# Weight low parts of the mixers' tiles: subtracted on VectorE at the end of a step, instead of on GpSimd beside it

## The reference, cut to what matters

```
h = rms_norm(x) * (1 + scale1) + shift1
h @ w_in -> A: pooling mixer (256), B: neighbourhood attention (8 heads x 64),
            C: gated linear attention (4 heads, dk 32, dv 64)
x = x + gate1 * concat(A, B, C) @ w_out
x = x + gate2 * swiglu(rms_norm(x) * (1 + scale2) + shift2)
```

## Time and profile before

| | |
|---|---|
| median of 3 runs | 1757.54 us (1757.44 to 1759.84) |
| the profiled execution | 1757.72 us; its span, first to last instruction, 1755.9 us |
| TensorE matmul | busy 1678.0 us (96%) |
| VectorE | 1038.4 us (59%) |
| GpSimd | 585.4 us (33%), of it 499.6 us the 196 subtractions of line 536 |
| ScalarE | 558.6 us (32%) |
| mean granted clock of TensorE | 0.98 |

### The profile page before, as it was taken

How to read it: one execution, slowest core, us unless ns; L and a number is a source line. 1 busy time by engine, 2 the same in 40 slices (tenths; PEclk the granted TensorE clock), 3 DMA queues, 4 the chain that set the end, 5 groups by cost and what they waited for, 6 DMA issues and landing times. The chain is left out here.

```text
span 1755.9 us, 29168 instructions
## 1 busy us (share of the span) xinstructions
PE 1678.0 (96%) x12024; PEld 1610.0 (92%) x12024; DVE 1038.4 (59%) x1885; ACT 558.6 (32%) x910; POOL 585.4 (33%) x281
## 2 busy tenths in 40 slices
PE   5979999999999999999999789998999999999998
PEld 4878889889999999999998678897999999999998
DVE  3477455758887488528777855566677713331342
ACT  4322455343322122112343225444332212221221
POOL 1135111126333334333452421111544333333332
PEclk9889899999999999999999989998999999999999
DMA  9234312112443344334331011210233222222223
GB/s 366 73 130 157 104 63 72 53 37 96 137 150 125 127 144 143 97 96 150 110 118 61 15 40 67 67 67 25 81 102 117 96 72 72 74 81 74 72 63 105
DMA packets 51306, 171.01 MB, mean 97 GB/s; under 512 B 6352, under 2 KB 9232, under 8 KB 51088
## 3 DMA queue, kind: packets, MB, share of 16 engines
q1 hardware_dynamic: 51216, 169.81, 29.5%
HBM read 165.98 MB, written 3.80 MB: 97 GB/s over the span
## 5 line engine op out<-in xcount | busy, mean ns | idle before, releaser
L536 POOL TENSOR_TENSOR w_lo<-w_raw,w_hi 128x1024 fp32r<-128x1024 f32 (+2 forms) x196 | 499.6, 2550 | 1083.9 <-ACT w_hi L637 1050.2
L637 ACT ACTIVATE w_hi<-w_raw 128x1024 fp32r<-128x1024 f32 (+2 forms) x194 | 200.3, 1033 | 674.2 <-PE acc L1367 609.9
L1367 PE MATMUL acc<-h_lo,w_hi 128*128 128x320 f32 (+1 forms) x1456 | 335.3, 312 | 0.0
L1367 PE MATMUL acc<-h_hi,w_hi 128*128 128x320 f32 (+1 forms) x1456 | 335.2, 312 | 0.0
L1367 PEld LDWEIGHTS acc<-h_hi,w_hi 128*128 128x128 f32 x1456 | 246.6, 190 | 1.6 <-issue 1.3
L1367 PEld LDWEIGHTS acc<-h_lo,w_hi 128*128 128x128 f32 x1456 | 246.3, 189 | 0.0
L1367 PE MATMUL acc<-h_hi,w_lo 128*128 128x320 f32 (+1 forms) x1456 | 230.3, 310 | 0.0
L1367 PEld LDWEIGHTS acc<-h_hi,w_lo 128*128 128x128 f32 x1456 | 219.7, 189 | 0.0
L1225 DVE SCALAR_TENSOR_TENSOR x<-acc,mods,x 128x320 f32<-128x320 f32 (+2 forms) x192 | 72.6, 434 | 221.9 <-PE acc L1367 200.9
L1367 PE MATMUL acc<-y_lo,w_hi 128*128 128x320 f32 x808 | 183.9, 309 | 0.0
L1367 PE MATMUL acc<-y_hi,w_hi 128*128 128x320 f32 x808 | 183.9, 309 | 0.0
(11 more groups left out here) (245 smaller groups left out, 2200.1 us busy)
## 6 DMA issues: line engine op xcount, KB each, us to landing
w_raw<-in_w SPq DMA_DIRECT2D x176, 512.0 KB, 3.5
mod_w<-in_w_ada SPq DMA_DIRECT2D x56, 512.0 KB, 4.5
w_gm<-in_w_ada SPq DMA_DIRECT2D x24, 512.0 KB, 4.6
bias<-in_bias SPq DMA_DIRECT2D x16, 576.0 KB, 4.6
w_ada<-in_w_ada SPq DMA_DIRECT2D x16, 512.0 KB, 13.6
w_raw<-in_w SPq DMA_DIRECT2D x16, 384.0 KB, 3.1
x<-in_x SPq DMA_DIRECT2D x4, 640.0 KB, 9.4
out_x<-x SPq DMA_DIRECT2D x8, 320.0 KB, 3.9
```

What stands on the lines that cost most here:

```text
L536: pool.tensor_tensor(w_lo[p][:, 0:n], raw[p][:, 0:n], w_hi[p][:, 0:n].bitcast(F32), ALU.subtract).then_inc(lo_made[p], 1)
L637: act.activation(w_hi[p][:, 0:n], raw[p][:, 0:n], ACT.Copy).then_inc(hi_made[p], 1)
L1367: mm = pe.matmul(acc[p][:, half, 0:m.shape[-1]], w[:, k * P:(k + 1) * P], m, start=w is w_hi[p] and k == 0 and part is hi, stop=w is w_lo[ ...
```

## The change

In the mixers `low` of tiles 8 to 23 leaves GpSimd's program and is put into VectorE's loop, in the steps that have a tile done, at the end of the step: only the pooling sums of steps 44 and 47 come behind it. It waits there for ScalarE's copy `w_hi` of the same tile, which ScalarE makes in the same step. Tiles 0 to 7 and those from 24 on stay on GpSimd. GpSimd's copies by head keep their order and their waits, without a subtraction between them.

```diff
--- before
+++ after
@@ GpSimd
-                for t in range(T_OUT):
+                for t in range(T_PAIR + 2):
                     low(t)
-                    if t == T_PAIR + 1:
-                        if l == 0:
-                            pool.wait_ge(late_in, 16 * NLATE)
-                        q_by_head(0)
-                        states_by_head(0)
-                        q_by_head(1)
-                    if t == T_PAIR + 2:
-                        for j in range(1, NP):
-                            if j + 1 < NP:
-                                q_by_head(j + 1)
-                            states_by_head(j)
-                low(T_OUT)
-                low(T_OUT + 1)
+                if l == 0:
+                    pool.wait_ge(late_in, 16 * NLATE)
+                q_by_head(0)
+                states_by_head(0)
+                q_by_head(1)
+                for j in range(1, NP):
+                    if j + 1 < NP:
+                        q_by_head(j + 1)
+                    states_by_head(j)
@@ VectorE
+                def low(t):
+
+                    p, n = t % 2, kts_of(t) * P
+                    dve.wait_ge(hi_made[p], slot_uses(l, t) + 1)
+                    dve.tensor_tensor(w_lo[p][:, 0:n], raw[p][:, 0:n], w_hi[p][:, 0:n].bitcast(F32),
+                                      ALU.subtract).then_inc(lo_made[p], 1)
...
+                    for n in tiles_done(g):
+                        low(T_PAIR + n + 2)
                     for i in range(2):
                         if g == 44 + 3 * i:
                             window_sums(i)
```

## The result

The kernel after takes 1738.63 us (median of 4 runs, 1737.44 to 1741.12) against 1757.76 for the kernel before on the same chip (4 runs, 1757.44 to 1759.84): ratio 0.9891, 95% interval 0.9873 to 0.9908. The forecast was 1737.0, with a range of 1730 to 1751. The profiled execution took 1737.4 with a span of 1735.7, 20.2 less than the 1755.9 of before.

What follows compares the result with a forecast made beforehand. TensorE was taken as the bound, full in attention, losing time to stalls on VectorE, held up by GpSimd's subtractions, and to half clock after them. 1757.7 - 4.0 - 3.5 - 3.2 - 10.0 = 1737.0 us; range 1730 to 1751.

Steps and rivals of the forecast that it cites:

- Step 9: Linear attention's norm, freed from GpSimd's subtractions, takes some 4.1 for 8.07; TensorE resumes 4.0 us earlier (layer 0), 3.5 (layer 1).
- the two stall terms: Shorter TensorE waits in linear attention: 4.0 us in layer 0, 3.5 in layer 1 after 0.5 off for step 4.
- Pooling sums: Before the first pooling product: window sums take 0.86 for 2.14; 1.6 us of the 3.22 stall per layer, 3.2 in all.
- The price of step 4: Linear attention: the low delays kk's multiply 2.1 us; 0.5 us left on layer 1's path, none in layer 0.
- The 32 lows: VectorE, mostly attention and pooling: 1.22 us each, 39 us more work; those of attention and pooling cost nothing, 32 us without cover.
- Rival two: Attention: VectorE becomes the bound, TensorE waits at each of 26 lows; slower, 1769 us; chance 0.06.
- Rival three: Step 7: head copies hold up the low, 2.44 for 1.22, step-4 wait back in full; 1741 to 1745; chance 0.15.
- DMA: Tile loads that wait for the lows: over 10 us sooner for tile 9, about a microsecond either way elsewhere; none late.
- Clock: Four half-clock stretches, in linear attention and pooling, recover 10.0 us of at most 15.3.
- rival one: Linear attention and pooling: stalls shrink but the clock does not recover; only 10.7 us come, 1747; chance 0.25.
- two thirds of the bound: Share taken of the 15.3 us that the four half-clock stretches cost at most: 10.0 us.

Runs made afterwards that it cites:

- e4: Kernel before, nothing moved to VectorE; GpSimd waits with the lows of tiles 9 and 10 until step 9's norm is done: 1747.1 us, ratio 0.9948.
- e5: Kernel after, plus three idle GpSimd subtractions with two SBUF inputs behind the head copies, where step 9's norm runs: 1750.6 us, ratio 0.9959.
- e6: Kernel after, plus six GpSimd memsets behind the last head copies, which write SBUF and do not read it: 1741.0 us, ratio 0.9900.
- e10: Kernel after once more, unchanged, with a second trace: 1739.3 us, ratio 0.9889.
- e8: Kernel after, lows of steps 4 and 7 put a step later on VectorE, those of 44 and 47 behind the window means: 1741.8 us, ratio 0.9905.
- e7: Kernel after, each low of steps 14 to 40 done twice on VectorE, once into a dead tile: 1739.6 us, ratio 0.9891.
- e11: Kernel after, plus twelve idle TensorE products in the wait for layer 1's second score product: 1736.4 us, ratio 0.9873.
- e12: Kernel of e9, plus seven idle TensorE products in the wait for layer 1's second score product: 1731.8 us, ratio 0.9860 to the kernel before.
- e1: Kernel before, only the lows of tiles 9 and 10 moved to VectorE (4 of 32): 1751.2 us, ratio 0.9963.
- e9: Kernel before, all lows on GpSimd, which waits with tiles 9, 10 for step 9's norm and 20, 21 for the window means: 1737.8 us, ratio 0.9876.

## Why the prediction was right, point by point

**Step 9: contention, 4.0 + 3.5.** Right, and shown from three sides: the norm is short when GpSimd is told to wait (e4), long again when it reads idle data (e5: 2.86 and 2.84), and short when it only writes (e6). The norm takes 4.09, forecast were some 4.1. The waits lost 8.8 (8.0 in e10, the second trace), against 8.0 in the two stall terms without the 0.5 that was taken off for step 4. In the kernel before neither of the two waits for the other there, so engines meet in SBUF too, and not only through semaphores. The Trainium skill's rule (SBUF — State Buffer, Who interferes with whom) has it so: a VectorE instruction with two SBUF inputs contends with a GpSimd instruction that reads SBUF, and not with one that only writes it. The traces agree on both halves, 2.86 us in e5 and 0.82 in e6.

**Pooling sums, 1.6 per layer.** Right: L1101 takes 0.86 in all four. The first bias add behind the first sum comes 0.95 sooner than the one before it had, the one behind the second 0.71 more: 1.66, against 0.9 and 0.7. TensorE's wait is 1.9, not 1.6: it lost 1.3 and not 1.6, since TensorE comes 0.3 sooner.

**The price of step 4, 0.5 in layer 1.** Right. The second score product starts 14.71 us after the first state update, where it was 12.63 (971.89 to 984.52): 2.1 later, as reckoned. The third starts after 23.95 instead of 23.53 (985.33 and 995.42): 0.4 of it is left. e8 undid this and gained nothing. What the prediction did not see is that VectorE is held up by GpSimd ahead of this wait too (last section).

**The 32 lows, nothing.** Right: 1.22 us each, attention unchanged at 127.9, and unchanged with nine more in each layer (e7). Rival two falls. Rival three's 2.44 did not come; a low beside the head copies takes 1.53 at most, and the wait that step 7's low brings is 0.7.

**DMA, nothing.** Right by the waits: no transfer of a tile is among those that grew, and TensorE's wait for GpSimd's lows went from 2.3 to 1.7.

**Clock, 10.0.** Too large: the parts show 5 to 8. That the total came out all the same was in part luck. At the four places that the term was added up from, the missing clock fell by 10.1 us, but they were not all that there was: the four parts had 27.2 us of it and kept 19.1. Of the 10.0, some 5.5 were for the poolings, where TensorE's busy time fell by 5.0 (5.1 in e10), and some 4.5 for linear attention, where it fell by 0.3 (0.1 in e10). The rest was filled by two waits that the sum does not have, for `mods` (2.8) and `gla_o` (1.5). The first is chance: in e10, the same kernel, it is 3.4 again.

The reason given for the term holds in part. That half clock goes with TensorE's standing still is shown for one wait (e11, e12). That only stalls of 3.22 us and more bring it is not so. In the kernel after, the clock is 1.00 from 982 to 990 us and then falls, with TensorE busy throughout and no wait since 976.09:

```profile
990.00:1000.00 10.00, 10.00 (x89) 8.84 (x89) 8.32 (x15) 5.11 (x7) 6.03 (x7) 0.83 0.08 13
```

Nor does the length of a wait tell how much follows: e8's 3.82 us brought more half clock than after's 5.89. The pooling wait of 1.9 us was followed by pooling parts of 53.9, 55.5 and 57.1 us in kernels with the same code there (after, e6, e7, e10). And rival one is what e1 showed, a stall of 8.0 us gone and in sum no clock back. What calls the half clock where TensorE does not wait stays open. The term should have stood with a spread of several us in every execution; two thirds of the bound fitted the poolings and not linear attention.

## What to carry to other kernels

Where an elementwise instruction takes three times as long in one place as in another, look at what the other elementwise engine reads just then. The cure need not be to move the work: a wait that keeps the two apart gave the same time here (e9). An engine with idle time under a full TensorE takes more work for nothing (e7); that a piece gains by standing behind what TensorE waits for next is not shown, since e8 did that and gained nothing. Time that a clock gives back should be forecast with a wide range, and a total that comes out right should be taken apart into busy and idle time before its terms are believed. A long TensorE wait that can't be removed may be worth filling with idle products: the medians fell by 2.9 us (e11) and 6.1 us (e12 against e9).

## What the runs showed that was not expected

The change cured the contention at two places, and a third is left: step 4 of linear attention, whose wait of 5.89 us is the longest in the mixers now. VectorE's arguments of kk and GpSimd's copies by head in layer 1 of the kernel after, in order of time:

```profile
965.87 3.39 DVE L999 TENSOR_TENSOR kk<-bcum 128x256 f32<-128x256 f32 x4
969.29 1.41 DVE L1003 TENSOR_SCALAR kk<-kk 128x1024 f32<-128x1024 f32 x1
...
976.32 1.42 DVE L999 TENSOR_TENSOR kk<-bcum 128x256 f32<-128x256 f32 x4
977.78 0.69 DVE L1003 TENSOR_SCALAR kk<-kk 128x1024 f32<-128x1024 f32 x1
```

```profile
965.11 2.69 POOL L559 TENSOR_TENSOR s_heads<-states,heads 128x256 f32<-128x256 f32 x4 [11.38 <-DVE states L1031]
967.76 2.40 POOL L546 TENSOR_TENSOR q_heads<-z,heads 128x512 f32<-128x512 f32 x2
```

Beside the copies the two lines take 4.8 us, 2.7 more than a chunk later, when GpSimd is idle. No run keeps the two apart here, so what that would be worth is not shown. The wait for `mods` in layer 0 hangs on the same thing: `mods` is made behind these two lines. They took 3.39 and 1.41 us in before and e10, with a wait of 3.6 and 3.4, and 2.54 and 0.69 in after, with a wait of 0.8. There the first score product ran wholly at half clock (2.58 us against 2.04 and 2.28), and GpSimd's second copy, which waits for it, began 0.9 us behind the first and not at once. So VectorE got through before it, and a slower clock made a shorter wait.

A shorter wait can be followed by more half clock: 14 us at 0.50 and 0.58 behind 3.82 us (e8), 5.9 us at 0.68 behind 5.89 (after). The same code gave 66.3, 69.1 and 70.4 us in linear attention of layer 1 (after, e10, and e7, which differs only later), at mean clocks of 0.87, 0.85 and 0.83. GpSimd is held up in its turn: its pair of subtractions takes 5.80 beside VectorE's norm and 4.71 behind it (e4).
